# Expert gathers on one core: the first head's scores taken without the norm in their chain, fourteen places in the first rounds of the gather ring, and a tile's second norm as one product on VectorE

## The reference, cut to what matters

```python
h2 = rms_norm(x, norm2_w) * (1.0 + scale2) + shift2     # 256 tokens x 1024
x  = x + gate2 * peer_ffn(h2, peer_wq, peer_subkeys, peer_u, peer_v)

def peer_ffn(h, ...):                                   # 8 heads, 16 picks of 16384 experts
    q = (hb @ peer_wq).reshape(B, 128, 8, 2, 128)
    s = einsum('bqhpd,hpnd->bqhpn', q, peer_subkeys)    # two lists of 128 scores a head
    vals, idx = top_k(s, 16)
    combo = vals[..., 0, :, None] + vals[..., 1, None, :]
    top_s, pos = top_k(combo, 16)                       # the 16 experts of a token and head
    g = softmax(top_s)
    a = gelu(einsum('bqhkd,bqd->bqhk', peer_u[expert], hb))
    return einsum('bqhk,bqhkd->bqd', g * a, peer_v[expert])
```

## Time and profile before

| | us |
|---|---|
| median of 3 runs | 1159.17 (1158.72 to 1159.63) |
| the profiled execution's own time | 1159.03 |
| span of its profile | 1157.0 |
| TensorE busy | 1044.9 (90%) |
| VectorE busy | 853.4 (74%) |
| ScalarE busy | 704.6 (61%) |
| GpSimd busy | 345.2 (30%) |
| gather queue's share of the 16 DMA engines' span | 55.9% |

### The profile page before, as it was taken

The page is one execution under the profiler, slowest core; times in us unless marked ns, Lnnn a source line. Parts: engine busy times, 40 slices in busy tenths (PEclk is TensorE's granted clock), DMA queues, the critical chain, the costliest instruction groups (busy, mean ns, idle before and its releaser), DMA issues.

```text
span 1157.0 us, 13373 instructions
## 1 busy us (share of the span) xinstructions
PE 1044.9 (90%) x4675; PEld 725.0 (63%) x4675; DVE 853.4 (74%) x1535; ACT 704.6 (61%) x1393; POOL 345.2 (30%) x367
## 2 busy tenths in 40 slices
PE   8999999999898978788877877799999999999997
PEld 6999987554454423333333323399888888888885
DVE  6998988766667666766677776546677768886776
ACT  3635835866776766666676666661458555577451
POOL 1001005555453544544544544555000000400000
PEclk9999999999999989988988998989999999999999
DMA  9987859999999999999999999999954654455540
GB/s 371 407 333 293 344 221 399 422 421 421 421 421 421 421 421 422 420 422 418 421 404 423 422 416 421 422 419 420 363 209 167 244 186 178 173 192 184 204 157 37
DMA packets 59557, 390.00 MB, mean 337 GB/s; under 512 B 6882, under 2 KB 7906, under 8 KB 15715
## 3 DMA queue, kind: packets, MB, share of 16 engines
q0 software_dynamic: 36864, 268.45, 55.9%
q1 hardware_dynamic: 21152, 120.10, 27.5%
q10 hardware_dynamic: 1474, 0.60, 0.2%
HBM read 388.08 MB, written 1.05 MB: 336 GB/s over the span
## 4 chain that ended last, share of the span: by engine, by line
PE 55%; DMA 28%; ACT 8%; DVE 6%; issue 2%; SPq 0%; POOL 0%; ACTq 0%; DVEq 0%; POOLq 0%
DMA rows<-in_peer_uv,work 17%; PE aux L1701 15%; DMA low_pairs<-in_peer_uv,work 8%; PE pj L1758 6%; PE pj L1760 6%; PE pj L1759 5%; PE pj L1816 5%; PE pj L1817 3%; PE aux L1707 3%; PE pj L1417 2%; ACT rows L1231 2%; PE pj L1419 2%; PE pj L1418 2%; PE aux L1676 2%; DVE rows L2230 2%
## 5 line engine op out<-in xcount | busy, mean ns | idle before, releaser
L1701 PE MATMUL aux<-rows,work 128*128 128x512 f32 x504 | 243.6, 633 | 46.2 <-ACT work L1247 46.0
L1701 PEld LDWEIGHTS aux<-rows,work 128*128 128x128 f32 x504 | 99.9, 202 | 178.1 <-issue 115.6
L1701 PE MATMUL aux<-low_pairs,work 128*128 128x512 f32 x356 | 176.0, 643 | 37.5 <-ACT work L1247 37.5
L992 POOL DMA_INDIRECT rows<-in_peer_uv,work x146 | 140.8, 964 | 231.0 <-PE aux L1701 148.4
L1231 ACT ACTIVATE rows<-rows 128x1024 f32<-128x1024 f32 x134 | 141.1, 1053 | 90.9 <-DVE rows L2230 90.5
L1701 PEld LDWEIGHTS aux<-low_pairs,work 128*128 128x128 f32 x356 | 71.6, 206 | 134.8 <-issue 84.1
L769 DVE TENSOR_TENSOR wlo<-wring,whi 128x1024 fp32r<-128x1024 f32 x98 | 121.0, 1250 | 32.6 <-ACT whi L763 31.8
L1231 ACT ACTIVATE low_pairs<-low_pairs 128x1024 f32<-128x1024 f32 x97 | 102.0, 1052 | 62.2 <-DVE low_pairs L2230 62.0
L992 POOL DMA_INDIRECT low_pairs<-in_peer_uv,work x101 | 97.3, 963 | 122.5 <-PE aux L1701 106.6
L763 ACT CAST whi<-wring 128x1024 fp32r<-128x1024 f32 x98 | 101.4, 1050 | 51.1 <-PE pj L1817 26.4
L2230 DVE TENSOR_TENSOR rows<-rows,aux 128x1024 f32<-128x1024 f32 x66 | 80.0, 1219 | 52.1 <-DMA rows<-in_peer_uv,work 51.6
(11 more groups left out here) (343 smaller groups left out, 2059.3 us busy)
## 6 DMA issues: line engine op xcount, KB each, us to landing
wring<-in_w SPq DMA_DIRECT2D x74, 1024.0 KB, 5.0
rows<-in_w_ada SPq DMA_DIRECT2D x46, 512.0 KB, 9.3
rows<-in_w SPq DMA_DIRECT2D x3, 1024.0 KB, 11.5
rows<-in_peer_uv,work POOLq DMA_INDIRECT x146, 12.7
low_pairs<-in_w SPq DMA_DIRECT2D x2, 1024.0 KB, 7.3
work<-in_late_rows SPq DMA_DIRECT2D x2, 1024.0 KB, 9.2
xT<-in_gate_rows SPq DMA_DIRECT2D x2, 1024.0 KB, 8.2
rows<-in_norm_rows SPq DMA_DIRECT2D x2, 1024.0 KB, 7.0
```

What stands on the lines that cost most here:

```text
L992: pool.indirect_dma_start(out=pair(n), out_offset=None, in_=a["peer_uv"], in_offset=bass.IndirectOffsetOnAxis(ap=expert[g % EXPERTS][:, j: ...
L1701: ins = mm(peer_sum[t][:, half(c)], diag[:, n % PICKS, :], pair(n)[:, D + c * 512:D + (c + 1) * 512], start=(n % (EXPERT_HEADS * PICKS) == ...
```

## The change

It has these parts.

1. **Head 0 of tile 0 is scored from `x * gain`.** ScalarE scales `x` by the gain as its chunks come (`gain_x`), into `xg`, whose column 129 is `shift2`. TensorE takes the query products from it, half of them before and half behind the last sums of squares of tile 0, and the key products of the queries and, apart, of the shift's column. VectorE takes tile 0's factor by token (`rstd_by_token`) and joins: scores times factor, plus the shift's part (`scores_of_head_0`).
2. **A tile's norm is one product** of 128 x 1024 with the factor spread over the chunks (`second_norm(t)`). Tile 0's stands ahead of the joining. Tile 1's stands behind the routing of the first eight picks. ScalarE multiplies tile 1 by the gain beforehand.
3. **Places.** Four rounds of 14, four of 12, then 10. Two places are new: ("low", 0) and ("low", 6). To free the latter, the last score keys are loaded into `extra` with the others of their kind. ("low", 7) is now the last place of the first round, pick 13.
4. **The last condition tiles** are taken in the output product's loop and right behind it.
5. **ScalarE's order** after the first query product: `gate_exps(0)` ahead of `score_out(0)`, four `sum_row` in place of two among the copies for head 1. `invert_gate(0)` moves between VectorE's second and third row products.
6. **Filler products** on TensorE (`keep_busy`, 4) go; 8 stand behind the first scores. The turning of tile 0 waits for its shift. `conv_std` becomes a count of `std_ready`.

```diff
-SLOTS, PAIRS = 12, 6
-PLACES = [("rows", 0), ("rows", 1), ("low", 2), ("low", 3), ("low", 4), ("low", 5), ("rows", 2), ("rows", 3), ("rows", 4), ("rows", 5), ("ring", 0), ("low", 7)]
-ROUNDS = [11] + [12] * 5 + [11] * 3
-LAST_ROUNDS = 10
+SLOTS, PAIRS = 14, 6
+PLACES = [("rows", 0), ("rows", 1), ("low", 2), ("low", 3), ("low", 4), ("low", 5), ("rows", 2), ("rows", 3), ("rows", 4), ("rows", 5),
+          ("low", 0), ("low", 6), ("ring", 0), ("low", 7)]
+LAST_ROUND = tuple(range(10))
+EARLY_ROUND, MIDDLE_ROUND = (0, 1, 2, 3, 4, 5, 10, 11, 9, 6, 7, 8, 12, 13), (0, 1, 2, 3, 4, 5, 10, 9, 6, 7, 8, 12)
+ROUNDS = [EARLY_ROUND] * 4 + [MIDDLE_ROUND] * 4
...
                 if n == OWN_EARLY:
-                    for own in (LAST_QUERY, *SUB_UNITS[:2]):
+                    for own in (LAST_QUERY, *SUB_UNITS):
                         load_unit(own)
...
-            sp.wait_ge(sums, 1 + NT)
-            load_unit(SUB_UNITS[2])
...
+                    if n == first_of("rows", 5):
+                        pool.wait_ge(last_ada_used, LAST_TILES)
+                    if n == first_of("low", 7):
+                        pool.wait_ge(queries, 8)
                     if n == first_of("rows", 2):
                         pool.wait_ge(queries, 2)
                     if n == first_of("rows", 3):
-                        pool.wait_ge(last_ada_used, LAST_TILES)
                         gate_diagonals(0)
                         pool.wait_ge(queries, 4)
...
-                    if n == first_of("low", 7):
-                        pool.wait_ge(queries, 8)
...
+            def gain_x(c):
+                nc.scalar.activation(xg[:, c, 0:P], xT[:, c, 0:P], ACT.Copy, scale=gain[:, c:c + 1]).then_inc(xg_ready, 1)
...
+            root(0)
+            for s in range(2):
+                act.wait_ge(early_products, s + 1)
+                nc.scalar.copy(pq[:, 0, s, 0:P + 1], aux[:, 4 + s, 0:P + 1]).then_inc(early_query_out, 1)
+            act.wait_ge(early_products, 3)
+            nc.scalar.copy(s_all[:, 0, :], aux[:, 1, 0:2 * KEYS]).then_inc(early_query_out, 1)
+            root(1)
             shift(0)
...
             score_query(0)
+            gate_exps(0)
             score_out(0)
-            gate_exps(0)
             for s in range(2):
+                sum_row(0, 2 * s)
+                sum_row(0, 2 * s + 1)
                 score_query(1, (s, ))
-                sum_row(0, s)
             score_out(1)
-            weigh_group(0, 0, 0, GROUP, summed=2)
+            weigh_group(0, 0, 0, GROUP, summed=GROUP)
...
-            out_sums(6, 7)
+            for s in range(2):
+                query_products(s, range(HC))
+            out_sums(6, 7, tiles=(0, ))
+            for s in range(2):
+                query_products(s, range(HC, KC)).then_inc(early_products, 1)
+            out_sums(6, 7, tiles=(1, ))
...
-            keep_busy(4, 1)
             early_scores_of_head_0()
-            pe.wait_ge(taken_dve, KC)
+            pe.wait_ge(early_query_out, 3)
+            for _ in range(8):
+                mm(aux[:, 1, 0:2 * P], ident[:, :], wsT[:, 0:2, :].rearrange("p g t -> p (g t)"), start=True, stop=True)
+            pe.wait_ge(taken_dve, KC + 1)
+            pe.wait_ge(h_ready, 2 * KC)
             turn_h2(0)
...
+            def second_norm(t):
+                ts = slice(t * P, (t + 1) * P)
+                dve.wait_ge(xg_ready, KC + 1 + t)
+                v.tensor_tensor(hT[:, :, ts], xg[:, :, 0:P] if t == 0 else hT[:, :, ts], rstd[:, ts].unsqueeze(1).broadcast_to([P, KC, P]),
+                                ALU.mult).then_inc(h_scaled, KC)
+            def rstd_by_token():
+                dve.wait_ge(std_ready, 3)
+                chain.link(v.tensor_tensor_reduce(s_left[:, 0, :], rstd[:, 0:P], ident[:, :], 1.0, 0.0, ALU.mult, ALU.add, rtok[:, :]))
+                chain.mark(v.reciprocal(rtok[:, :], rtok[:, :]))
+            def scores_of_head_0():
+                dve.wait_ge(early_query_out, 3)
+                dve.wait_ge(early_products, 4)
+                chain.wait()
+                v.scalar_tensor_tensor(s_all[:, 0, :], aux[:, 0, 0:2 * KEYS], rtok[:, :], s_all[:, 0, :], ALU.mult, ALU.add).then_inc(early_scores_out, 1)
...
-            second_norm()
+            last_ada_tile(1)
+            last_ada_bias()
+            dve.wait_ge(taken_dve, KC + 1)
+            rstd_by_token()
+            second_rstd(0)
+            second_norm(0)
+            scores_of_head_0()
...
-            route_in_two()
-            last_ada_tiles()
-            invert_gate(0)
+            route_first()
+            second_rstd(1)
+            second_norm(1)
+            route_rest()
             dve.wait_ge(h2_turned, 1)
             for j in range(GROUP):
+                if j == 2:
+                    invert_gate(0)
                 dot(0, j)
```

More of the change, by code:

```diff
@@ L285 @@
 LAST_PICK = NT * EXPERT_HEADS * PICKS - 1
-PLACE_OF = [k for size in ROUNDS for k in range(size)]
-PLACE_OF += [n % LAST_ROUNDS for n in range(LAST_PICK + 1 - len(PLACE_OF))]
+PLACE_OF = [k for places in ROUNDS for k in places]
+PLACE_OF += [LAST_ROUND[n % len(LAST_ROUND)] for n in range(LAST_PICK + 1 - len(PLACE_OF))]
 def picks_before(n):
@@ L367, in sem @@
             return ctx.enter_context(nc.semaphore(name))
-        extra = sb("extra", [P, 3 * D])
+        extra = sb("extra", [P, 3 * D + 512])
         wring = sb("wring", [P, RING, WUNIT])
@@ L476, in build @@
         assert w3.at <= 4096
+        XG_AT = 4096 + EXPERT_HEADS * 2 * KEYS
+        xg = work[:, XG_AT:XG_AT + KC * (P + 1)].rearrange("p (c n) -> p c n", n=P + 1)
         count16 = sb("count16", [P, PICKS], I32)
@@ L1165, in _, with gain_x_of_tile_1 @@
             halves_ = [slice(t * P, (t + 1) * P) for t in range(NT)]
+            def gain_x(c):
+                nc.scalar.activation(xg[:, c, 0:P], xT[:, c, 0:P], ACT.Copy, scale=gain[:, c:c + 1]).then_inc(xg_ready, 1)
+            def gain_x_of_tile_1(*chunks):
+                for c in chunks:
+                    ins = nc.scalar.activation(hT[:, c, P:T], xT[:, c, P:T], ACT.Copy, scale=gain[:, c:c + 1])
+                return ins
             for c in range(KC - 1):
@@ L1200, in score_out @@
                                aux[:, h % 2, first * 2 * KEYS:].rearrange("p (n k) -> p n k", k=2 * KEYS)).then_inc(scores_out, 1)
-            shift(0)
[L1203 to L1206, removed]
-            nc.scalar.copy(s_all[:, 0, :], aux[:, 0, 0:2 * KEYS]).then_inc(early_scores_out, 1)
+            root(0)
[5 more added lines that the diff above has]
+            root(1)
+            shift(0)
             shift(1)
@@ L1460, in token_major @@
                             ins.then_inc(proj, 1)
-            def keep_busy(n, b):
-                pe.wait_ge(const_ready, 13)
-                for _ in range(n):
-                    mm(aux[:, b, 0:2 * P], ident[:, :], wsT[:, 0:2, :].rearrange("p g t -> p (g t)"), start=True, stop=True)
             pe.wait_ge(const_ready, 3)
@@ L1643, in _, with out_sums @@
                 ins.then_inc(proj, 1)
-            def out_sums(*columns):
+            def out_sums(*columns, tiles=range(NT)):
                 for k in columns:
-                    for t in range(NT):
+                    for t in tiles:
                         pe.wait_ge(squares, k + 1 if k < KC - 1 else KC + t)
@@ L1657, in _, with query_products @@
             out_sums(4, 5)
-            out_sums(6, 7)
+            query_of_head_0 = w_slot(FIRST_HEADS[0])
+            w_wait(pe, FIRST_HEADS[0])
+            def query_products(s, chunks):
+                for k in chunks:
+                    pe.wait_ge(xg_ready, k + 2)
+                    ins = mm(aux[:, 4 + s, 0:P + 1], query_of_head_0[:, k, s * P:(s + 1) * P], xg[:, k, :], start=(k == 0), stop=(k == KC - 1))
+                return ins
+            for s in range(2):
[4 more added lines that the diff above has]
+            out_sums(6, 7, tiles=(1, ))
             def turn_h2(t):
@@ L2277, in combine, with route_first @@
                 return z
-            def route_in_two():
-                first, rest = slice(0, FIRST_ROUTED), slice(FIRST_ROUTED, PICKS)
-                lists = [s_all[:, 0, s * KEYS:(s + 1) * KEYS] for s in range(2)]
+            first, rest = slice(0, FIRST_ROUTED), slice(FIRST_ROUTED, PICKS)
+            lists = [s_all[:, 0, s * KEYS:(s + 1) * KEYS] for s in range(2)]
+            def route_first():
                 dve.wait_ge(early_scores_out, 1)
```

83 lines of the change are left out of this document (43 added, 40 removed).

## The result

The changed kernel takes 1173.38 us (median of 4, 1172.81 to 1174.64) against 1158.95 (4 executions, 1158.54 to 1159.63): ratio 1.0125, 95% interval 1.0108 to 1.0143. It is 14.4 us slower; 1173.8 was predicted. The profiled execution took 1172.88, with a span of 1171.1.

The account below looks back on a forecast made before the run. The prediction took the gather stream to bound the kernel: pick 13, held until `queries` 8, lands 14.6 us later, which takes the profiled execution's 1159.03 to 1173.6; with 0.14 for the median, 1173.8, range 1169.5 to 1177.

Parts of the forecast that it names:

- The stream of gathers as the clock of the stage: Expert stage: 256 gathers, 2.49 us apart, set its length; a microsecond of later start is a microsecond of the kernel.
- Head 0's chain: From the last piece of `x` to routing: ends at 166.6, a gain of 2.4 us, first issue at 170.1.
- Tile 1's norm: Moved behind the routing of eight picks: tile 1's query product starts at 174.4, 3.1 us later than before.
- TensorE's list to `queries` 8: From tile 1's query product on TensorE: 45.3 us, not shortened by the change, so `queries` 8 comes at 219.7.
- the lower bound: Earliest `queries` 8: 43 us after a start at 173.3, less 1.8 for the clock: 214.5, making +9.4.
- The fourteenth place: Pick 13 in ("low", 7) waits on GpSimd for `queries` 8: issued 219.9, landing 226.1, DMA idle about 17 us.
- The sum: Pick 13 lands at 226.1 against 211.5 before, 14.6 later, and all later work moves with it: 1173.8.
- Picks 8 to 12 are summed meanwhile.: Behind the held pick: picks 8 to 12, landed long before, are summed while nine gathers go out at once.
- The early start drops out of this sum.: Gather stream: the earlier first issue doesn't count; only the time of `queries` 8 does.
- the earlier start is what remains: Rival: the wait at pick 13 is met in time, `queries` 8 by 203; -2.4, so 1156.8; chance 0.05.
- The clock: TensorE's low clock at tile 1's first query product: 1.8 us either way; rival beyond 1177, chance 0.06.

Follow-up runs that it names:

- e3_norm: Experiment 7: the changed kernel with tile 1's norm back ahead of the routing, held place still at pick 13; 1174.54 us, ratio 1.0137.
- e1_late: The changed kernel with ("low", 7) left out of the first round, its wait at pick 26; 1159.00 against 1159.02 us, ratio 0.9995.
- e8_late_fill: e1_late with eight more filler products on TensorE before tile 1's first query product; 1156.97 against 1159.24 us, ratio 0.9981.
- e2_p17: As e1_late, but ("low", 7) is the fifth place of the second round, pick 17; 1165.63 us, ratio 1.0050.
- e7_no_places: The changed kernel with places, rounds and GpSimd's waits of before (12 places, first round 11); 1161.51 us, ratio 1.0018.
- e11_act: The changed kernel with ScalarE's list of before, the norm left where the change puts it; 1173.59 us, ratio 1.0120.
- after: The changed kernel itself, against the kernel before; 1173.38 against 1158.95 us, ratio 1.0125.
- e5_fill: The changed kernel with eight more filler products before tile 1's first query product, nothing else; 1171.60 us, ratio 1.0106.
- e12_old_fill: e7_no_places with the eight more filler products of e8_late_fill; 1159.37 against 1158.99 us, ratio 1.0005.
- e4_late_norm: e1_late with tile 1's norm back ahead of the routing of the first eight picks; 1158.47 against 1159.24 us, ratio 0.9990.
- e10_norm_act: e3_norm with ScalarE's list of before as well; 1170.81 against 1159.53 us, ratio 1.0100.
- e6_places: The kernel before with only the change's places, rounds, score keys in extra and GpSimd's waits; 1170.91 us, ratio 1.0104.

## Why the prediction was right, point by point

- **The stream of gathers as the clock of the stage.** Right. The table shows that everything behind the held pick moves with it.
- **Head 0's chain.** Predicted: routing from 166.6, first issue 170.1. Measured: 166.42 and 169.97. The steps were less exact than the sum. TensorE's last key product ended at 165.30 + 0.39 = 165.69, not at 166.6, and VectorE's side, called shorter, was as long: its norm product ended at 164.57 + 1.22 = 165.79, and the joining (0.49) ran at once behind it.
- **Tile 1's norm.** One product, taken as 1.22 between 1.22 and 2.19: 1.23. Tile 1's query product at 174.4: 174.38.
- **TensorE's list to `queries` 8.** 45.3 assumed unchanged, 45.6 measured, so 219.7 became 220.02. (The products named in the prediction add up to 43.7, not 43. The 45.3 is read from the rows, so only the lower bound is touched, by 0.7.)
- **The fourteenth place.** Issue 219.9, landing 226.1; measured 220.29 and 225.83. The landing came 5.54 behind the issue, shorter than any before; the next one came 3.14 after it, not 2.49. That these two errors cancel is luck.
- **The sum.** Pick 14 landed at 228.97, 15.0 later than its 213.95 in the stream of before. The last issue, at 815.40, is 14.5 later than before, 800.9, and the profiled executions differ by 13.9. The stream gave 1.1 back from 595 to 605 (421 against 374) and lost 0.7 from 605 to 700 (417 against 420), and what follows the last issue was 0.6 shorter. The forecast had nothing for any of these; that they come to so little is luck too.
- **"Picks 8 to 12 are summed meanwhile."** Wrong, without a price. Their diagonals are made by GpSimd, and `gate_diagonals(8)` stands behind the blocked gather. ScalarE waited 9.83 us for it, TensorE 5.28, and picks 8 to 11 were summed from 225.30 on. The nine gathers from pick 13 to pick 21 go into places that were free by then, and GpSimd issued them one behind the other from 220.29 to 232.25. Only pick 22, issued at 233.50, needs the sum of pick 8, so the stream had no use for these sums before. Behind the waiting instruction stood this as well as the gathers, and I had listed only the gathers. By the order of the code it also bounds how far forward the held place could go: at pick 12 the diagonals of picks 4 to 7 would stand behind the wait that needs their sums, and the wait would never end. That was not run.
- **"The early start drops out of this sum."** Right for the changed kernel. Experiment 7 shows its limit: with the query products earlier, ScalarE's new order ties them to the landing of pick 3. I had costed that order at nothing, for cover that the late norm gives and that is gone in e3_norm.
- **The rival "the earlier start is what remains"** needed `queries` 8 by 203. It came at 220. With the held place out of the way it isn't automatic either: 0.0 in e1_late, and 2.3 us in e8_late_fill once the fillers hold the clock.
- **The clock.** The bounds had 1.8 us for it in each direction. In the changed kernel's profile the rest of 3.86 us cost no more than that of 1.93 before (5.47 against 5.41), but e1_late, e2_p17 and e7_no_places had 6.4 to 6.5. That the changed kernel's profile lay at the low end, as the sum assumes, is luck of about 1 us.

## What to carry to other kernels

When transfers are issued in order into places that come free at different times, the place that comes free last must go where the work already under way covers its wait; price it as the landing of the held transfer against its turn, and the head start before it counts for nothing. List everything behind a wait on its engine, helpers for other engines too. And where a stream has only a microsecond to spare, a rest of TensorE of a few us just ahead of the products that feed it decides whether a gain is seen: fill it.

## What the runs showed of the hardware

**The clock after a rest.** The same rest of 3.86 us before tile 1's product was followed by a product of 5.46 (e11_act), 5.47 (after), 6.41 (e7_no_places), 6.43 (e2_p17) and 6.50 us (e1_late). The granted clock was 0.50, the 1.2 GHz level, in 176 to 178 of the last four. With fillers in place of the rest (e8_late_fill, e5_fill, e12_old_fill) the product took 3.84, and e8_late_fill had 1.00, the 2.4 GHz level, from 172 to 188. In e2_p17 TensorE rested 2.35 us more behind this product, and the clock was low once more, 0.50 in 184 to 186, so head 1's product took 8.38 instead of 7.07. After a rest of 0.58 (e3_norm, e4_late_norm, e10_norm_act) the product took 3.84. The Trainium skill, "TensorE: Matmul & The Clock Gate", section "Part 1: The HAM clock gate", says that the point of transition varies from run to run of one kernel. These rows are single executions of five kernels that do the same up to this product. Their spread of 1.0 us fits the sentence, but no run here shows it for one kernel.

**A restart of the stream.** After an empty stretch the first gather landed 5.54 us behind its issue (220.29 to 225.83), where the shortest had been 5.8, and the second 3.14 behind the first instead of 2.49; in e6_places it was 222.84 and 226.72, 3.88 apart. All seven kernels that ran dry show it: the first landing 5.40 to 5.69 behind its issue, the second 2.99 to 3.94 behind the first. Why the second is late was not tried.
